# A ninth resident expert tile, and products of constants in TensorE's waits, in a four-stage transformer kernel

## The chip, the cores and the metric
One core of one Trainium2 chip runs the whole kernel in one launch. The metric is the time of an execution in microseconds, the median of several runs. Views of the trace count from the start of the profiled execution's span.

## The reference
Two blocks, in fp32, on 256 tokens of width 1024. The first has two layers, and each is a mixer and a mixture of experts:

```python
for layer in range(DEPTH):                       # DEPTH = 2
    h = rms_norm(x, norm_mix_g[layer])
    ...                                          # layer 0: even_mixer, layer 1: odd_mixer
    x = x + mix
    h = rms_norm(x, norm_ffn_g[layer])
    x = x + hier_moe(h, moe_w_group[layer], moe_b_group[layer], ...)
```

`hier_moe` picks one of 4 groups and the best 2 of its 8 experts for each token. There are 32 experts of hidden width 512 in a layer: silu(h W_gate) * (h W_up), times W_down, weighted by the gates. The second block has two layers of a hybrid mixer and a gated feed-forward part (hyb0, ffn0, hyb1, ffn1), and a last norm.

## The kernel before
The stages run one after another: even, moe0, odd, moe1, hyb0, ffn0, hyb1, ffn1, fin. Each engine has its own program, and semaphores with names such as "even mixed3" order them (`K.after(name)`). All weights stream from HBM through tiles of 128 x 4096 fp32 (2048 KB), in one fixed order (`chunk_table`), issued by SyncE (`sp_program`, L3270) strictly in turn: before a tile SyncE waits until the slot's last holder is free, and everything later in the order waits behind it.

An expert stage has 8 groups q of four experts. A group has 12 tiles, in this order: g{q}_0 to 3 (gate), u{q}_0 to 3 (up), d{q}_0 to 3 (down), so a stage has 96. Tile 0 is g0_0, tile 8 is d0_0, tile 95 is d7_3. The ring has six slots; while the ring goes round, a tile waits for the one six ring places ahead of it. Two tiles of each expert stage, g0_3 and u0_0, have places of their own at the end of the arena, the large work area, which is free only when the mixer before is nearly done (`aside`: "even mixed3", "odd z3"). The router's weights (`_r`) have another place.

For each group TensorE gathers the chosen tokens (at most 32 an expert) by a one-hot product (L804), multiplies gate and up tiles (L828, 16 matmuls a tile on quarters of the array), transposes, multiplies the down tiles (L853), and scatters the result back into x with four products (L860). Before group 0 comes the router: transposes of x (L717), logits (L785), a chain of small DVE operations that ends in "chosen", positions (L789 to L791), the first one-hot, and then gather(0). The PSUM banks go round in turn (`bank`).

An expert with more than 32 tokens is served by the general path (`over_pe` and its like), behind a branch at the end of the stage, which needs the normed features in `HT`. They are made in group 1 for every input, by `features_pe` and `features_act`.

After an expert stage the next norm transposes x (`norm_pe`, L641), and in hyb0 ACT cuts the first weights (L2323) before it copies the features (L2405).

Of the kernel before, what the change touches and what calls it, by code (L numbers as in the profile page):

```python
# [188 lines left out]
class Kernel:  # L189
    def __init__(self, nc, ctx, Wd, Pd, x_in, out_d, stages):  # L190
# [51 lines left out]
        for i, (name, k, n) in enumerate(self.chunks):  # L242
            if name in aside:
                area, landed, freed = aside[name]
                self.slot.append((landed, area[:, 0:k * n]))
                self.freed.append(freed)
                self.landing[name] = (landed, 16)
                continue
            if name == "moe0_g0_0":
                order, turn = [3, 4, 5, 2, 0, 1], 0  # L250
            elif name == f"moe1_g{NE // 4 - 1}_0":
                order, turn = [1, 3, 4, 2, 0, 5, 1, 2, 0, 4, 5, 3], 0
            elif i == first:
                order, turn = list(range(FEW)), 0
            s, turn = order[turn % len(order)], turn + 1
            was, nth = held.get(s, (None, 0))
            self.freed.append(was and "free " + was)
            if name == "moe0_g0_3" or (s == 2 and was == "lora"):
                self.freed[-1] = "even mixed3"
            held[s] = (name, nth + 1)  # L260
            r, o = (ring, s) if s < FEW else (ring2, s - FEW)
            self.slot.append((self.s_slot[s], r[:, o * SLOT:o * SLOT + k * n]))
            self.place[name] = s
            self.landing[name] = (self.s_slot[s], 16 * (nth + 1))
# [11 lines left out]
    def aside(self, sem):  # L276

        out = {}
        for st, before, done in (("moe0", "even", "even mixed3"), ("moe1", "odd", "odd z3")):
            if st in self.stages:  # L280
                done = done if before in self.stages else None
                for i in range(2):
                    at = NA - 2 * SLOT + i * SLOT
                    out[f"{st}_" + ("g0_3", "u0_0")[i]] = (self.AR[:, at:at + SLOT], sem(f"s_{st}_{i}"), done)
                r = self.CS_T[:, 1440:1728] if st == "moe0" else self.AR[:, 12300:12588]
                out[st + "_r"] = (r, sem(f"s_{st}_r"), done if st == "moe1" else None)
        return out
# [337 lines left out]

def norm_pe(K, pe, st):
    S, b, ident = K.sig[st, "pe"], norm_bufs(K, st), K.par("ident", 0, 128)
    of, p = K.high if K.stage_before(st) == "odd" else K.banks, {}
    for t in range(2):  # L630
        for k in range(0, 8, 2):
            name = f"{st} nT{k}"
            if t == 0:
                p[k] = bank(K, pe, name, of)
            if k == 0:
                pe.wait_ge(*K.after(f"{st} xv{t}"))
            elif k == 4:
# [36 lines left out]
def moe_bufs(K, st):  # L674
    b = norm_bufs(K, st)
    buf = Area(K.AR, b.end, s5_top())
    b.L = buf(2, 36)
# [6 lines left out]
    b.SQs = [buf(2, 4, CAP) for _ in range(2)]  # L684
    b.XGs = [buf(8, 4 * CAP) for _ in range(2)]
    b.SG = [buf(512) for _ in range(2)]
# [64 lines left out]

def features_pe(K, pe, st):

    S, b, ident = K.sig[st, "pe"], norm_bufs(K, st), K.par("ident", 0, 128)
    for k in range(0, 8, 2):
        p = bank(K, pe, f"{st} nT{k}")
        for kk in (k, k + 1):
            for t in range(2):
                o = (kk - k) * 256 + t * 128
                r = pe.transpose(p[:, o:o + 128], b.xn[:, t, kk * 128:(kk + 1) * 128], ident)  # L760
        r.then_inc(*S.up(f"{st} nT{k}"))

def features_act(K, a, st):
    S, g = K.sig[st, "act"], "g_" + st
    for k in range(0, 8, 2):
        p = K.banks[f"{st} nT{k}"]
        a.wait_ge(*K.after(f"{st} nT{k}"))
        for kk, names in ((k, []), (k + 1, [f"{st} nT{k} read"])):
            o = (kk - k) * 256  # L770
            a.activation(K.HT[:, kk, :], p[:, o:o + 256], ACT.Copy, scale=K.par(g, kk)).then_inc(*S.up(*names))

def moe_pe(K, pe, st):
# [5 lines left out]
    for t in range(2):  # L780
# [5 lines left out]
        r.then_inc(*S.up(f"{st} r{t}", f"free {st}_r"))  # L786
    p = bank(K, pe, st + " pos")
    pe.wait_ge(*K.after(st + " chosen"))
    pe.matmul(p[:, 0:32], tri, b.Sf[:, 0, :], start=True, stop=True)  # L789
# [22 lines left out]
    for q in range(NE // 4):  # L812
# [28 lines left out]
        if q < NE // 4 - 1:  # L841
            gather(q + 1)
        if q == 1:
            features_pe(K, pe, st)
        ys = [bank(K, pe, f"{st} y{q}{n}") for n in range(2)]
        pe.wait_ge(*K.after(f"{st} hT{q} read"))
        for k in range(4):
# [3 lines left out]
            for n in range(2):  # L851
                for j in range(4):
                    r = pe.matmul(ys[n][32 * j:32 * j + 32, :], b.HTr[u][:, k, j * CAP:(j + 1) * CAP],  # L853
                                  w[:, j, n * 512:(n + 1) * 512], start=k == 0, stop=k == 3)
            r.then_inc(*S.up("free " + name, f"{st} y{q}"))
        for t in range(2):
            for n in range(2):
                pe.wait_ge(*K.after(f"{st} y{q}{n} read"))
                p = bank(K, pe, f"{st} o{q}{n}{t}")
                pe.matmul(p, b.SC[u][:, t, :], b.YS[u][:, n, :], start=True, stop=True).then_inc(  # L860
# [4 lines left out]
def moe_act(K, a, st):  # L865
# [7 lines left out]
    for q in range(NE // 4):  # L873
# [6 lines left out]
        a.activation(b.SC[u], half2(K.banks[f"{st} sT{q}"][:, 0:256]), ACT.Copy).then_inc(*S.up(f"{st} sT{q} read"))  # L880
        if q == 1:
            features_act(K, a, st)
        next(beside, None)
# [197 lines left out]
def over_end(K, e, l):  # L1081
    dve, act, pe, _ = K.over[l]
    e.wait_ge(dve, 3 * NE)
    e.wait_ge(act, NE)
    e.wait_ge(pe, 8 * NE)

def over_pe(K, pe, st, l, flag, hint):
    b, (dve, act, done, dma), HT = over_bufs(K), K.over[l], K.HT
    with over_path(K, pe, st, "pe", flag, hint):  # L1090
        for e in range(NE):
            pe.wait_ge(dma, 16 * 12 * (e + 1))
# [19 lines left out]
def over_act(K, a, st, l, flag):  # L1112
    b, (dve, done, pe, dma) = over_bufs(K), K.over[l]
    with over_path(K, a, st, "act", flag):
        for e in range(NE):
            a.wait_ge(pe, 8 * e + 4)
            if e:
# [5 lines left out]
def over_dve(K, v, st, l, flag):  # L1123

    b, (done, act, pe, dma), G = over_bufs(K), K.over[l], kept_gates(K, l)
    with over_path(K, v, st, "dve", flag):
        for e in range(NE):
            v.wait_ge(act, e + 1)
            v.tensor_tensor(b.hi, K.ps[:, 4:8, 0:256], b.sg, MUL).then_inc(done, 1)
            for t in range(2):  # L1130
                v.wait_ge(pe, 8 * e + 6 + 2 * t)
                v.scalar_tensor_tensor(out=K.X[:, t, :], in0=K.ps[:, 2 * t:2 * t + 2, :].rearrange("p n d -> p (n d)"),
# [4 lines left out]
def over_sp(K, sp, st, l):  # L1137
    b, (dve, act, pe, dma) = over_bufs(K), K.over[l]
    first = K.index[st + "_g0_0"]
    with over_path(K, sp, st, "sp", over_flag(K, sp, st, l)):  # L1140
        for e in range(NE):
            q, j = e // 4, e % 4
            if e:
                sp.wait_ge(pe, 8 * e)
            for part, dst in ((0, b.wg), (4, b.wu), (8, b.wd)):
# [18 lines left out]
def even_bufs(K):  # L1164
    b, cv, buf = Box(), K.consts("even_c"), Area(K.AR)
    b.M = buf(14, 256)
    b.LD, b.AA, b.GG, b.KK = (buf(4, 256) for _ in range(4))
    b.OT, b.YT = buf(8, 256), buf(4, 256)
    b.R, b.K2, b.VV = b.M[:, 0:4, :], b.M[:, 4:8, :], b.M[:, 8:12, :]
# [16 lines left out]
    two.PT, two.PV, two.VS = b.R[:, 0, :], b.K2[:, 0, :], b.VV[:, 0, :]  # L1186
    two.bh_at, two.bh = 14 * 256 + 12 * 256, b.KK[:, 0, :]
    two.BS, two.CS = b.AA[:, 0, :], b.LD[:, 0, :]
# [2161 lines left out]
def pool_program(K, g):  # L3350
# [3 lines left out]
    for st in K.stages:  # L3354
        nxt = K.stage_after(st)
        if st[:3] in ("moe", "ffn") and nxt is not None and nxt + "_c" in K.coffs:
            before = K.stage_before(st)
            if before is not None:
                for sem, n in K.ends(before):
                    g.wait_ge(sem, n)  # L3360
            load_consts(K, g, nxt)

# [244 lines left out]
```

## Time and profile before

| | |
|---|---|
| median of 3 runs | 2744.92 us (2742.62 to 2747.47) |
| profiled execution, its own time | 2738.76 us |
| its span | 2737.0 us |
| TensorE (matmuls) busy | 2300.2 us, 84% |
| weight loads, DVE, ACT busy | 1749.6, 1263.6, 941.2 us |
| moved by DMA | 663.18 MB, 242 GB/s mean |
| mean granted TensorE clock | 0.936 of full speed |

A busy share is an average over stages: the expert stages lie at about 273 to 732 us and 910 to 1370 us of the span, and there the views of single stretches have to be read. A clock of 0.50 is 1.2 GHz, one of 1.00 is 2.4 GHz.

### The profile page before, as it was taken

The page shows a single profiled execution, that of the slowest core. Times are in us where ns is not written, and L with a number is a line of the kernel's source. Part 1 is how long each engine was busy: PE and PEld are TensorE (multiplying, and loading weights), DVE is VectorE, ACT ScalarE, POOL GpSimd, SP SyncE. Part 2 cuts the span into 40 slices and gives each one's busy share as a digit, 9 for nine tenths or more (in the row PEclk, how much of TensorE's full clock was granted, in tenths as well). Part 3 has the DMA queues.
Part 4 walks back from the last instruction along what each step waited for, and adds up shares of the span by engine and source line. Part 5 has one row for each costly group of instructions (what it writes and reads, how often), then busy time and mean ns, then how long its engine had stood idle before and what let it go on. Part 6 is the DMA issues. An engine that isn't in the chain of part 4 may idle for free.

```text
span 2737.0 us, 37411 instructions
## 1 busy us (share of the span) xinstructions
PE 2300.2 (84%) x16364; PEld 1749.6 (64%) x16364; DVE 1263.6 (46%) x1914; ACT 941.2 (34%) x1382; POOL 2.4 (0%) x8
## 2 busy tenths in 40 slices
PE   7877766666696866666599999999999999999999
PEld 6666322211274421122189998999979999989997
DVE  2575321222294211111066568765545656866554
ACT  3133100000113200000055557745444555764543
POOL 0000000000000000000000000000000000000000
PEclk9998888988897988878899999999999999999999
DMA  6101999999905599999954443445544434334452
GB/s 274 62 1 74 400 428 428 428 427 428 416 17 248 244 428 427 427 428 428 427 198 170 149 178 141 154 154 199 182 172 154 167 146 185 130 148 160 180 185 100
DMA packets 47818, 663.18 MB, mean 242 GB/s; under 512 B 5280, under 2 KB 5536, under 8 KB 7584
## 3 DMA queue, kind: packets, MB, share of 16 engines
q1 hardware_dynamic: 47072, 657.39, 59.7%
q8 instruction: 132, 2.16, 0.3%
q0 software_dynamic: 576, 3.32, 0.3%
q14 instruction: 38, 0.31, 0.0%
HBM read 659.64 MB, written 1.05 MB: 241 GB/s over the span
## 4 chain that ended last, share of the span: by engine, by line
PE 54%; DMA 29%; DVE 9%; ACT 7%; issue 2%; SPq 0%; DVEq 0%; ACTq 0%
DMA ring<-w_dram 28%; PE ps L2346 7%; PE ps L2348 7%; PE ps L2347 7%; PE ps L1818 3%; PE ps L1231 2%; PE ps L828 2%; PE ps L2599 2%; PE ps L2600 2%; PE ps L2601 2%; PE ps L853 2%; ACT r L2323 2%; PE ps L3201 1%; PE ps L3199 1%; PE ps L3200 1%
## 5 line engine op out<-in xcount | busy, mean ns | idle before, releaser
L2334 DVE TENSOR_TENSOR r<-ring,r 128x1024 fp32r<-128x1024 f32 (+1 forms) x392 | 505.1, 1301 | 345.9 <-ACT r L2323 345.3
L2346 PE MATMUL ps<-r 128*128 128x256 f32 x2112 | 608.0, 288 | 15.1 <-DVE arena L2933 5.7
L2347 PE MATMUL ps<-r 128*128 128x256 f32 x2112 | 598.2, 283 | 0.0
L2348 PE MATMUL ps<-r 128*128 128x256 f32 x2112 | 598.0, 283 | 0.0
L2323 ACT ACTIVATE r<-ring 128x1024 fp32r<-128x1024 f32 (+1 forms) x392 | 429.5, 1116 | 269.1 <-PE ps L2348 131.8
L828 PE MATMUL ps<-ring,arena 128*32 128x512 f32 x1984 | 297.4, 731 | 207.0 <-DMA ring<-w_dram 206.9
L2346 PEld LDWEIGHTS ps<-r 128*128 128x128 f32 x2112 | 405.5, 192 | 22.8 <-issue 6.7
L2347 PEld LDWEIGHTS ps<-r 128*128 128x128 f32 x2112 | 405.7, 192 | 0.2
L2348 PEld LDWEIGHTS ps<-r 128*128 128x128 f32 x2112 | 405.5, 192 | 0.0
L828 PEld LDWEIGHTS ps<-ring,arena 128*32 128x32 f32 x1984 | 62.1, 121 | 433.0 <-DMA ring<-w_dram 221.2
L1030 DVE TENSOR_TENSOR arena<-ps,arena 128x512 f32<-128x512 f32 x16 | 11.1, 692 | 472.7 <-PE ps L828 472.7
L853 PE MATMUL ps<-ring,arena 128*32 128x512 f32 x1024 | 145.4, 702 | 81.1 <-DMA ring<-w_dram 80.1
L2599 PE MATMUL ps<-arena,r 128*128 128x256 f32 x512 | 145.4, 284 | 0.0
L2600 PE MATMUL ps<-arena,r 128*128 128x256 f32 x512 | 143.9, 281 | 0.0
L853 PEld LDWEIGHTS ps<-ring,arena 128*32 128x32 f32 x1024 | 30.5, 119 | 177.2 <-DMA ring<-w_dram 121.8
L2601 PE MATMUL ps<-arena,r 128*128 128x256 f32 x512 | 143.8, 281 | 0.0
L878 ACT ACTIVATE arena<-ps 128x512 f32<-128x512 f32 x16 | 9.6, 597 | 292.9 <-PE ps L828 292.9
L880 ACT ACTIVATE arena<-ps 128x256 f32<-128x256 f32 x16 | 6.1, 383 | 285.4 <-PE ps L834 285.4
L885 ACT ACTIVATE arena<-ps 128x512 f32<-128x512 f32 x16 | 9.6, 597 | 262.7 <-PE ps L853 262.7
L1038 DVE COPY arena<-ps 128x512 f32<-128x512 f32 x16 | 11.1, 692 | 192.4 <-PE ps L853 192.4
L2599 PEld LDWEIGHTS ps<-arena,r 128*128 128x128 f32 x512 | 96.5, 188 | 1.2 <-issue 0.7
L2600 PEld LDWEIGHTS ps<-arena,r 128*128 128x128 f32 x512 | 96.5, 188 | 0.1
(433 smaller groups left out, 3416.6 us busy)
## 6 DMA issues: line engine op xcount, KB each, us to landing
ring<-w_dram SPq DMA_DIRECT2D x305, 2048.0 KB, 23.7
arena<-w_dram SPq DMA_DIRECT2D x4, 2048.0 KB, 21.9
ring<-w_dram SPq DMA_DIRECT2D x4, 1024.0 KB, 4.9
cst<-w_dram POOLq DMA_DIRECT2D x2, 973.0 KB, 8.2
x<-x_dram SPq DMA_DIRECT2D x1, 1024.0 KB, 7.9
ring<-w_dram SPq DMA_DIRECT2D x2, 512.0 KB, 13.5
out_dram<-x SPq DMA_DIRECT2D x4, 256.0 KB, 2.0
ring<-w_dram SPq DMA_DIRECT2D x1, 768.0 KB, 15.8
```

The costliest lines, as they stand in the source:

```text
L828: r = pe.matmul(p[32 * j:32 * j + 32, :], xg[:, k, j * CAP:(j + 1) * CAP], w[:, kk * 4 + j, :], start=k == 0, stop=k == 7)
L853: r = pe.matmul(ys[n][32 * j:32 * j + 32, :], b.HTr[u][:, k, j * CAP:(j + 1) * CAP], w[:, j, n * 512:(n + 1) * 512], start=k == 0, stop=k ...
L1231: x = pe.matmul(o(c), l[:, c, :], r(c), start=True, stop=True)
L1818: r = pe.matmul(p[:, n * 256:(n + 1) * 256], w[:, k, c0 + n * 128:c0 + n * 128 + 128], rhs[:, k, :], start=k == 0, stop=k == n_k - 1)
L2323: a.activation(hi, w, ACT.Copy).then_inc(*S.up(f"hi {s}"))
L2334: v.tensor_tensor(lo, w, hi.bitcast(F32), SUB).then_inc(*S.up(f"lo {s}", *(["free " + name] if last else [])))
L2346: pe.matmul(out, hi[:, k, :], K.HH[:, k, :], start=k == 0, stop=False)
L2347: pe.matmul(out, hi[:, k, :], K.HL[:, k, :], start=False, stop=False)
L2348: r = pe.matmul(out, lo[:, k, :], K.HH[:, k, :], start=False, stop=k == 7)
L2599: pe.matmul(o, hi[:, k, :], b.YH[:, kk, :], start=kk == 0 and n == 0, stop=False)
L2600: pe.matmul(o, hi[:, k, :], b.YL[:, kk, :], start=False, stop=False)
L2601: r = pe.matmul(o, lo[:, k, :], b.YH[:, kk, :], start=False, stop=kk == 15 and n == 1)
```

## The change
Each expert stage gets a third arena place, for u0_1. In moe0 it is free with the others; in moe1 it waits for "odd av3". To make room, the arena areas of the even stage are put in another order, and the gathered inputs `XGs` move from the arena to `HT`. The general path, which found its features in `HT`, makes them itself, and `features_pe` and `features_act` go. The router's weights of moe1 go to the space of the constants of the odd stage, behind "odd roped1", and GpSimd waits for the router's matmuls before it loads the constants of hyb0. The ring order of moe1's last group is another. `warm` multiplies the identity by constants into a bank that is written again later; it is called three times before "chosen", twice after each of the first three down tiles of the last group, and in the norms before the waits.

```diff
             elif name == f"moe1_g{NE // 4 - 1}_0":
-                order, turn = [1, 3, 4, 2, 0, 5, 1, 2, 0, 4, 5, 3], 0
+                order, turn = [2, 0, 1, 3, 4, 5, 2, 0, 1, 4, 5, 3], 0
...
-                for i in range(2):
-                    at = NA - 2 * SLOT + i * SLOT
-                    out[f"{st}_" + ("g0_3", "u0_0")[i]] = (self.AR[:, at:at + SLOT], sem(f"s_{st}_{i}"), done)
-                r = self.CS_T[:, 1440:1728] if st == "moe0" else self.AR[:, 12300:12588]
-                out[st + "_r"] = (r, sem(f"s_{st}_r"), done if st == "moe1" else None)
+                heads = "odd av3" if done == "odd z3" else done
+                for name, at, when in (("g0_3", NA - 2 * SLOT, done), ("u0_0", NA - SLOT, done), ("u0_1", NA - 3 * SLOT, heads)):
+                    out[f"{st}_{name}"] = (self.AR[:, at:at + SLOT], sem(f"s_{st}_{name}"), when)
+                r, when = (self.CS_T[:, 1440:1728], None) if st == "moe0" else (self.CS_T[:, 0:288], done and "odd roped1")
+                out[st + "_r"] = (r, sem(f"s_{st}_r"), when)
...
+def warm(K, pe, out):
+
+    n = out.shape[1]
+    pe.matmul(out, K.par("ident", 0, 128), K.par("ident", 0, n), start=True, stop=True)
...
@@ norm_pe
             if k == 0:
+                if t == 0 and K.stage_before(st):
+                    warm(K, pe, p[0][:, 0:512 if after_moe(K, st) else 256])
+                elif t and K.stage_before(st):
+                    warm(K, pe, p[6][:, 128:256])
+                    warm(K, pe, p[6][:, 384:512])
                 pe.wait_ge(*K.after(f"{st} xv{t}"))
...
@@ moe_bufs
-    b.XGs = [buf(8, 4 * CAP) for _ in range(2)]
+    b.XGs = [K.HT[:, i:i + 4, :].rearrange("p a (b c) -> p (a b) c", b=2) for i in (0, 4)]
...
@@ moe_pe
     p = bank(K, pe, st + " pos")
+    for _ in range(3):
+        warm(K, pe, p)
     pe.wait_ge(*K.after(st + " chosen"))
...
-        if q == 1:
-            features_pe(K, pe, st)
         ys = [bank(K, pe, f"{st} y{q}{n}") for n in range(2)]
+        if q == NE // 4 - 1:
+            spare = bank(K, pe, f"{st} o{q}00")
...
             r.then_inc(*S.up("free " + name, f"{st} y{q}"))
+            if q == NE // 4 - 1 and k < 3:
+                warm(K, pe, spare)
+                warm(K, pe, spare)
...
-                p = bank(K, pe, f"{st} o{q}{n}{t}")
+                p = spare if q == NE // 4 - 1 and t == n == 0 else bank(K, pe, f"{st} o{q}{n}{t}")
...
@@ moe_act
-        if q == 1:
-            features_act(K, a, st)
...
@@ over_pe
+        xn = norm_bufs(K, st).xn
+        for k in range(8):
+            for t in range(2):
+                r = pe.transpose(K.ps[:, k // 2, k % 2 * 256 + t * 128:k % 2 * 256 + t * 128 + 128],
+                                 xn[:, t, k * 128:(k + 1) * 128], K.par("ident", 0, 128))
+        r.then_inc(done, 1)
+        pe.wait_ge(act, 8)
...
@@ even_bufs
-    b.LD, b.AA, b.GG, b.KK = (buf(4, 256) for _ in range(4))
-    b.OT, b.YT = buf(8, 256), buf(4, 256)
+    b.OT = buf(8, 256)
+    b.LD, b.AA, b.GG = (buf(4, 256) for _ in range(3))
+    kk, b.KK, b.YT = buf.at, buf(4, 256), buf(4, 256)
...
@@ pool_program
+            if st == "moe1":
+                g.wait_ge(*K.after("free moe1_r"))
             load_consts(K, g, nxt)
```

## Rows read from the trace of the kernel before

**Rows 1.** The page, 40 equal slices of the span: rate of all DMA.

```profile
GB/s 274 62 1 74 400 428 428 428 427 428 416 17 248 244 428 427 427 428 428 427 198 170 149 178 141 154 154 199 182 172 154 167 146 185 130 148 160 180 185 100
```

**Rows 2.** The page, the chain that ended last, by line.

```profile
DMA ring<-w_dram 28%; PE ps L2346 7%; PE ps L2348 7%; PE ps L2347 7%; PE ps L1818 3%; PE ps L1231 2%; PE ps L828 2%; PE ps L2599 2%; PE ps L2600 2%; PE ps L2601 2%; PE ps L853 2%; ACT r L2323 2%; PE ps L3201 1%; PE ps L3199 1%; PE ps L3200 1%
```

**Rows 3.** The chain in order of time, moe0: start us, us, what.

```profile
343.96 1.97 PE ps L828 x16
345.94 27.34 DMA ring<-w_dram
...
728.06 3.59 PE ps L853 x16
```

**Rows 4.** Windows, moe0's start: busy us (instructions) by engine, clock, DMA share, GB/s.

```profile
288.00:290.00 2.00, 2.00 (x20) 1.39 (x22) 1.08 (x3) 0.00 (x0) 0.00 (x0) 1.00 0.18 74
290.00:292.00 2.00, 2.00 (x24) 0.65 (x20) 0.87 (x5) 0.00 (x0) 0.00 (x0) 1.00 0.00 0
292.00:294.00 2.00, 2.00 (x24) 0.62 (x20) 0.00 (x0) 0.00 (x0) 0.00 (x0) 1.00 0.98 254
```

**Rows 5.** Timeline of SyncE's DMA issues: start us, us, what, how many.

```profile
260.42 0.80 SPq L3270 DMA_DIRECT2D arena<-w_dram  x2
...
839.33 0.80 SPq L3270 DMA_DIRECT2D ring<-w_dram  x2
...
906.62 35.07 SPq L3270 DMA_DIRECT2D ring<-w_dram  x8
```

**Rows 6.** Timeline of the odd stage, "odd roped1" and "odd av3".

```profile
839.30 1.23 DVE L2134 TENSOR_TENSOR arena<-arena 128x1024 f32<-128x1024 f32 x1
...
887.77 0.39 PE L1926 MATMUL ps<-arena 128*128 128x128 f32 x2
```

**Rows 7.** Windows, the end of odd and moe1's start, columns as in rows 4.

```profile
884.00:906.00 22.00, 21.29 (x55) 9.84 (x54) 2.13 (x3) 8.45 (x15) 0.00 (x0) 1.00 0.00 0
...
916.00:918.00 2.00, 0.00 (x0) 0.00 (x0) 2.00 (x16) 0.21 (x1) 0.00 (x0) 0.50 1.04 439
...
920.00:922.00 2.00, 1.17 (x6) 1.19 (x6) 1.74 (x10) 0.01 (x1) 0.00 (x0) 0.50 0.34 141
922.00:924.00 2.00, 2.00 (x12) 2.00 (x11) 0.61 (x4) 0.00 (x0) 0.00 (x0) 0.50 0.00 0
...
926.00:928.00 2.00, 2.00 (x22) 1.61 (x24) 0.86 (x2) 0.00 (x0) 0.00 (x0) 1.00 0.00 0
928.00:930.00 2.00, 2.00 (x25) 0.55 (x20) 1.10 (x5) 0.00 (x0) 0.00 (x0) 1.00 0.03 8
930.00:932.00 2.00, 2.00 (x24) 0.62 (x20) 0.00 (x0) 0.00 (x0) 0.00 (x0) 1.00 0.81 188
```

**Rows 8.** Timeline, group 1 of moe0, then the start of moe1.

```profile
357.04 3.74 PE L804 MATMUL ps<-arena 128*128 128x128 f32 x32
...
361.25 3.02 ACT L771 ACTIVATE ring<-ps,pp 128x256 f32<-128x256 f32 x8 [4.79 <-PE ps L760]
...
918.55 0.61 PE L789 MATMUL ps<-arena,pp 128*128 128x32 f32 x2 [3.27 <-DVE arena L970]
...
920.84 6.23 PE L804 MATMUL ps<-arena 128*128 128x128 f32 x32 [0.83 <-issue]
...
927.37 5.36 PE L828 MATMUL ps<-ring,arena 128*32 128x512 f32 x48
```

**Rows 9.** Timeline, last tiles of moe0 and moe1, and the norm behind.

```profile
728.06 3.53 PE L853 MATMUL ps<-ring,arena 128*32 128x512 f32 x16 [2.97 <-DMA ring<-w_dram]
...
1360.89 1.92 PE L853 MATMUL ps<-ring,arena 128*32 128x512 f32 x16 [3.01 <-DMA ring<-w_dram]
1365.86 3.32 PE L853 MATMUL ps<-ring,arena 128*32 128x512 f32 x16 [3.04 <-DMA ring<-w_dram]
...
1376.40 2.73 PE L641 MATMUL ps<-pp,arena 128*128 128x128 f32 x12 [0.72 <-ACT arena L576]
...
1376.77 1.04 ACT L2323 ACTIVATE r<-ring 128x1024 fp32r<-128x1024 f32 x1
```

More of the change, by code:

```diff
@@ L675, in moe_bufs @@
     b = norm_bufs(K, st)
-    buf = Area(K.AR, b.end, s5_top())
+    buf = Area(K.AR, b.end, NA - 3 * SLOT)
     b.L = buf(2, 36)
@@ L749, in turn_act @@
     scale_act(K, a, st, 1)
[L752 to L771, printed above, removed]
 def moe_pe(K, pe, st):
@@ L1083, in over_end @@
     e.wait_ge(dve, 3 * NE)
-    e.wait_ge(act, NE)
-    e.wait_ge(pe, 8 * NE)
+    e.wait_ge(act, 8 + NE)
+    e.wait_ge(pe, 1 + 8 * NE)
 def over_pe(K, pe, st, l, flag, hint):
@@ L1114, in over_act @@
     with over_path(K, a, st, "act", flag):
+        a.wait_ge(pe, 1)
+        for k in range(8):
+            a.activation(K.HT[:, k, :], K.ps[:, k // 2, k % 2 * 256:k % 2 * 256 + 256], ACT.Copy,
+                         scale=K.par("g_" + st, k)).then_inc(done, 1)
         for e in range(NE):
-            a.wait_ge(pe, 8 * e + 4)
+            a.wait_ge(pe, 8 * e + 5)
             if e:
@@ L1127, in over_dve @@
         for e in range(NE):
-            v.wait_ge(act, e + 1)
+            v.wait_ge(act, e + 9)
             v.tensor_tensor(b.hi, K.ps[:, 4:8, 0:256], b.sg, MUL).then_inc(done, 1)
             for t in range(2):
-                v.wait_ge(pe, 8 * e + 6 + 2 * t)
+                v.wait_ge(pe, 8 * e + 7 + 2 * t)
                 v.scalar_tensor_tensor(out=K.X[:, t, :], in0=K.ps[:, 2 * t:2 * t + 2, :].rearrange("p n d -> p (n d)"),
@@ L1142, in over_sp @@
             q, j = e // 4, e % 4
-            if e:
-                sp.wait_ge(pe, 8 * e)
+            sp.wait_ge(pe, 8 * e + 1)
             for part, dst in ((0, b.wg), (4, b.wu), (8, b.wd)):
@@ L1186, in even_bufs @@
     two.PT, two.PV, two.VS = b.R[:, 0, :], b.K2[:, 0, :], b.VV[:, 0, :]
-    two.bh_at, two.bh = 14 * 256 + 12 * 256, b.KK[:, 0, :]
+    two.bh_at, two.bh = kk, b.KK[:, 0, :]
     two.BS, two.CS = b.AA[:, 0, :], b.LD[:, 0, :]
```

## The prediction
> **What bounds the kernel now.** I read the page first. Its line of DMA rates shows 428 GB/s, the highest figure of the line, in slices 6 to 10 and 15 to 20: the two expert stages [rows 1]. The chain that ended last names the transfers into the ring as its largest single item, 28% of the span [rows 2]. The chain in order of time shows why: through an expert stage it goes from a tile's landing to some 2 us of matmuls, which free a ring slot, and from that slot to the landing of the tile that takes it, 27.34 us and six tiles later [rows 3]. The matmuls of tile 17 of the first expert stage start at 343.96, those of the last, tile 95, at 728.06: 384.10 / 78 = 4.92 us for one tile of 2048 KB. So an expert stage ends when its last tile lands, plus a tail. Its length is the number of tiles left to stream when streaming begins, times 4.92 us. Outside these stages the rate is far below 428, and there a tile can be fetched for nothing.
>
> Then I looked at how each stream begins. With windows of 2 us, moe0's shows a hole: 74 GB/s at 288 to 290, nothing until 292, 254 after it [rows 4]. Counting what is missing from 428, the hole is 2 x (354 + 428 + 174) / 428 = 4.47 us. All free slots are full, and tile 8 waits for the slot of tile 0, which TensorE has only just begun to read. In moe1 the hole is larger: 141, then 0, 8 and 188 GB/s between 920 and 932 [rows 7], or 2 x (287 + 3 x 428 + 420 + 240) / 428 = 10.4 us.
>
> **The ninth tile.** Before, six ring slots and two arena slots hold tiles 0 to 7 when the stage begins. After, tile u0_1 has an arena slot of its own, so tile 8 (d0_0) gets a ring slot whose holder was done before the stage.
>
> moe0: the new slot is free with "even mixed3", the event at which SyncE issues the two arena tiles at 260.42 [rows 5]; the tile for the last slot goes once even_out1 is used. Its 4.9 us of transfer follow the eighth tile's and fill a hole of 4.47 us. Tile 9 then waits for tile 0's slot, as tile 8 did, and finds it free while the ninth tile is still on its way. The stream gains what the hole is worth: 4.47 us. An earlier release of the slot adds nothing here, as no hole is left.
>
> moe1: the router's weights move from the arena to the space of the cosines and wait for "odd roped1". The DVE operation behind that name starts at 839.30 and takes 1.23 us [rows 6]; SyncE issues the two odd_out tiles, which are queued ahead, at 839.33 [rows 5], and they keep the DMA busy for 9.8 us, so that this wait and all tiles queued behind it cost nothing. The ninth slot waits for "odd av3", and the two matmuls before it start at 887.77 [rows 6]. Everything behind u0_1 in SyncE's queue (u0_2, u0_3, d0_0, d0_1) waits with it. From 884 to 906 the DMA moves nothing [rows 7], so u0_1 and u0_2 are in by about 898; u0_3 and d0_0 follow the slots of the odd_out tiles from 906.62 on [rows 5], where two tiles went before. The hole stays where it is, and one tile fewer comes after it: 4.92 us. The constants of hyb0, which GpSimd now holds back until the router's matmuls are over (about 4 us), share the DMA ahead of the hole; at 128 x 1946 x 4 bytes, 1.0 MB, they need 2.3 us of it.
>
> **What is removed.** The general path's own transposes and copies take 16 transposes and 8 ACT operations out of group 1 of each expert stage, and the gathered inputs move to the buffer that they used. Group 1 lies in the middle of the DMA stream, where TensorE waits some 3 us for each tile: 0. If the stream were no cover, it would be worth the 3.02 us of the copies [rows 8] a stage; no part of the general path runs in this profile. The changed order of ring slots in moe1's last group asks each tile to wait for one at least five places ahead (four before): 0.
>
> **The products of constants.** One such product, 128x512, should cost what a 128x512 pass of the tiles' matmuls suggests: 48 matmuls that use a quarter of the array together take 5.36 us [rows 8], four side by side 0.45 us, so 0.45 us at full clock and twice that at half. All stand in front of a wait. Three ahead of "chosen": TensorE idles 3.27 us there [rows 8], they need 1.3 to 2.7. Two after each of the last group's first three down tiles: a wait of some 3 us [rows 9], they need 0.9 to 1.8. A tile's 16 matmuls take 1.8 us at full clock (5.36 / 3) and 3.6 at half, and 3.6 + 1.8 = 5.4 is over 4.92: if the clock stayed down, each tile would delay the next by 0.5, or 1.4 us a stage. In the norms they need 0.2 to 0.9 us beside idle time of the same size: 0, at worst 0.5 us in all.
>
> Can they pay? In moe1 the clock is 0.50 from 916 to past 922 and 1.00 from 926 on [rows 7]. In this time the 32 gather matmuls (L804) take 6.23 us; the same 32 of a later group take 3.74 [rows 8]. Up to 2.5 us earlier, tile 0's slot is free, the hole in moe1 ends, and the whole stream with it. But three products end 2 us before "chosen" at full clock, and whether they hold the clock up until then no row shows; I take 1.0, with 0 and 2.5 as bounds. In the tails, the last tile's 16 matmuls take 3.53 us (moe0) and 3.32 (moe1), against 1.92 for the tile at 1360.89 [rows 9]: the clock fell in the 3 us of waiting. This time is behind the last landing and fully exposed, 1.6 + 1.4 = 3.0 us. Here the products cut the idle stretch from 3 to 2 us at full clock, and at half clock they leave hardly any, so that the clock should be up at the last tile more often than not; I take 2.0 of 3.0, bounds 3.0 and -2.8 (the delay above). After the tail, moe1's twelve slow transposes (2.73 us) end while ACT is still busy with the first cut (1.04 us from 1376.77) and what follows it in order [rows 9]: 0.
>
> The Trainium skill, "TensorE: Matmul & The Clock Gate", section "HAM oscillation — how this bites in real kernels", describes this pattern: matmuls shorter than the wait for the next slice lose the clock and each burst starts slow. The trace agrees in part: [rows 9] has both a fast and a slow burst after the same wait. By that page alone all 3.0 us of the tails would be there to win, and the sum would be 1.0 us larger.
>
> **The sum.** 4.47 + 4.92 + 1.0 + 2.0 = 12.4 us off the profiled execution, whose own time is 2738.76 us (span 2737.0). That execution is 6.2 us below the median of the three runs, 2744.92, and 3.9 below the fastest; tile counts and holes don't depend on it, so I take 12.4 off the median: 2732.5.
>
> **Rivals.**
> *The transfers alone pay.* What holds the clock is not what the products do, or it starts at another place in each execution and the profiled one was an unlucky one. For it: in [rows 7] the clock stays at 0.50 through 922 to 924, in which TensorE is busy all the time. 4.47 + 4.92 = 9.4 us: 2735.5. The same page, section "Part 1: The HAM clock gate (the "warmup" mystery)", says that the number of slow matmuls varies between runs of one kernel, which is this rival's rule.
> *The tile pays in one stage only.* In one stage its load doesn't move the first landing after the hole (in moe1 because the queue behind "odd av3" runs late; that costs from 909 on, when 4 tiles at 4.9 us and 2.3 us of constants no longer end by 931; in moe0 because the fifth and sixth transfers slip). 888 is 21 us ahead of that. Gain 4.5 to 5 us plus 0 to 3: about 2738.5, at the edge of what can be measured.
> *Slower: the stream itself loses pace.* Place: the 174 tiles after the holes. One more part of the arena is written while DVE and ACT use the rest, and a tile that takes longer shifts everything behind it. Price: 174 x 0.1 = 17.4 us, 8 us slower on balance; it decides from 0.054 us a tile (4.92 to 4.974) where the gain of 9.4 is gone. Against it: the rate is the same 427 to 428 in every slice of both stages, with tiles going to ring and arena alike [rows 1]. 2753.
>
> **How the numbers follow.** Forecast (transfers plus some of the clock): 0.60. Transfers alone: 0.24. One stage only: 0.10. More of the clock than its bound in the profile: 0.03. Slower stream: 0.03. Low end: 9.4 + 2.5 + 3.0 = 14.9 us gives 2730.0; the runs of before lie up to 2.5 us from their median, and with the rare fourth case I go to 2726.5. High end: the transfers alone less 2.8 us of delays is 2738.3, and 1.7 of scatter (both extremes together are rare) makes 2740, which also takes in most of the one-stage case. 0.2% is 5.5 us, about what a measurement of this kernel can tell from no change. Faster by more: the first, second and fourth case, and a little of the third: 0.88. Within it: 0.09. Slower: 0.03.
>
> **What would show it.** In windows of 2 us, 288 to 294 must have the full rate in moe0; in moe1 a hole must remain, 8 to 10 us long, with nine tiles ahead of it, and two more tiles must move between 888 and 898. The last tile of moe0 must start some 4.5 us earlier after its stage's start, that of moe1 5 to 7 us. Gather matmuls near 3.7 us and last tiles near 1.9 would show the products at work. If the router's matmuls start as before and the last landing isn't earlier, the first step is wrong; if all is as described and the total isn't, a later stage gave it back.

## The result and the profile after

The changed kernel takes 2726.8 us (median of 4 runs, 2725.96 to 2727.97), the kernel before 2743.77 us beside it (4 runs, 2742.6 to 2747.47): a ratio of 0.9936, with a 95% interval of 0.9919 to 0.9953. The profiled execution takes 2726.56 us, 12.2 less than the profiled one of before (2738.76). The forecast took 12.4 us off the earlier median of 2744.92, for 2732.5; the median fell by 17.0 against the one beside it.

First the page of the kernel after: the rate of DMA in 40 slices and the chain by line, for [rows 1, 2].

```profile
GB/s 276 62 1 78 427 428 428 427 428 427 399 16 241 303 428 428 428 427 428 428 177 155 159 186 124 155 177 179 186 170 155 184 130 186 141 138 166 175 186 101
DMA ring<-w_dram 27%; PE ps L2349 7%; PE ps L2350 7%; PE ps L2351 7%; PE ps L819 3%; PE ps L1821 3%; PE ps L1234 2%; PE ps L2602 2%; PE ps L2603 2%; PE ps L2604 2%; PE ps L844 2%; ACT r L2326 1%; PE ps L3204 1%; PE ps L3202 1%; PE ps L3203 1%
```

The expert stages run at the same 427 to 428 GB/s, and the transfers into the ring are still the largest item. The windows of the two starts, for [rows 4, 7] with the same columns:

```profile
286.00:288.00 2.00, 2.00 (x24) 0.65 (x20) 0.94 (x5) 0.00 (x0) 0.00 (x0) 1.00 1.02 434
288.00:290.00 2.00, 2.00 (x24) 0.56 (x20) 0.00 (x0) 0.00 (x0) 0.00 (x0) 1.00 1.02 434
290.00:292.00 2.00, 2.00 (x24) 0.61 (x20) 0.00 (x0) 0.00 (x0) 0.00 (x0) 1.00 1.00 418
292.00:294.00 2.00, 2.00 (x24) 0.65 (x20) 0.00 (x0) 0.60 (x1) 0.00 (x0) 1.00 0.99 418
...
880.00:890.00 10.00, 9.86 (x27) 4.63 (x26) 0.75 (x1) 6.03 (x8) 0.00 (x0) 1.00 0.89 349
...
916.00:918.00 2.00, 1.99 (x18) 2.00 (x19) 1.64 (x10) 0.00 (x0) 0.00 (x0) 1.00 0.00 0
918.00:920.00 2.00, 2.00 (x21) 2.00 (x19) 0.84 (x2) 0.00 (x0) 0.00 (x0) 1.00 0.03 8
920.00:922.00 2.00, 2.00 (x22) 0.75 (x25) 1.81 (x6) 0.00 (x0) 0.00 (x0) 1.00 0.00 0
922.00:924.00 2.00, 2.00 (x24) 0.52 (x16) 0.00 (x0) 0.00 (x0) 0.00 (x0) 1.00 0.61 123
924.00:926.00 2.00, 2.00 (x24) 0.65 (x20) 0.00 (x0) 0.00 (x0) 0.00 (x0) 1.00 0.94 369
```

In moe0 the hole of 288 to 294 is gone. In moe1 a hole remains: from 914 to 926 what is missing from 428 adds up to 9.1 us. And the DMA moves 4.2 MB, two tiles, between 880 and 892, in a stretch where before it moved nothing (the odd stage begins some 7 us earlier now, so these times answer to 887 and later in [rows 7]). TensorE's timeline, for [rows 8, 9]; L630 is `warm`, L795 the gather, L819 the gate and up tiles, L844 the down tiles, L854 the scatter:

```profile
275.18 4.52 PE L630 MATMUL ps<-pp 128*128 128x512 f32 x6
279.54 0.30 PE L780 MATMUL ps<-arena,pp 128*128 128x32 f32 x2
...
281.11 3.81 PE L795 MATMUL ps<-arena 128*128 128x128 f32 x32 [0.82 <-issue]
...
721.55 1.92 PE L844 MATMUL ps<-ring,arena 128*32 128x512 f32 x16 [1.06 <-DMA ring<-w_dram]
...
733.88 1.35 PE L1849 MATMUL ps<-ring 128*128 128x256 f32 x5 [1.22 <-ACT ring L675]
...
901.83 1.91 PE L728 MATMUL ps<-pp,x 128*128 128x128 f32 x16
904.87 4.99 PE L774 MATMUL ps<-cst,ring 128*128 128x36 f32 x32 [1.13 <-DVE arena L893]
909.67 4.93 PE L630 MATMUL ps<-pp 128*128 128x512 f32 x6
914.43 0.30 PE L780 MATMUL ps<-arena,pp 128*128 128x32 f32 x2
...
916.01 3.81 PE L795 MATMUL ps<-arena 128*128 128x128 f32 x32 [0.82 <-issue]
...
1353.88 1.92 PE L844 MATMUL ps<-ring,arena 128*32 128x512 f32 x16 [1.04 <-DMA ring<-w_dram]
1356.52 3.70 PE L854 MATMUL ps<-arena 128*128 128x512 f32 x8 [0.72 <-ACT arena L877]
1362.95 1.13 PE L630 MATMUL ps<-pp 128*128 128x512 f32 x2 [2.73 <-issue]
```

The gather and both last tiles run at full clock (3.81, 1.92, 1.92 us). Two waits are new. The router's matmuls of moe1 (L774) wait 1.13 us for a DVE operation of the odd stage, and the first projection of odd (L1849) 1.22 us for ACT. Before, neither waited for these:

```profile
740.75 1.53 PE L1846 MATMUL ps<-ring 128*128 128x256 f32 x6 [0.40 <-DVE ring L653]
...
909.86 1.92 PE L717 MATMUL ps<-pp,x 128*128 128x128 f32 x16
911.62 3.66 PE L785 MATMUL ps<-arena,ring 128*128 128x36 f32 x32
```

And at 1362.95 TensorE has idled 2.73 us with "issue" as the reason: it waited for nothing that the profile shows.

**By stages.** The points are starts on TensorE's timeline: T a stage's first transposes, g0 tile 0's matmuls, "last" the last down tile, "next" the first matmul after the norm behind it. "even" runs from the landing of x to moe0's T. Each cell is in us from the profile of that execution. The expert sum is the four columns T to last and last to next of both stages.

| execution | span | even | moe0 T-g0 | T-last | last-next | moe1 T-g0 | T-last | last-next | expert sum |
|---|---|---|---|---|---|---|---|---|---|
| before | 2737.0 | 262.5 | 17.44 | 456.35 | 12.69 | 17.51 | 456.00 | 14.14 | 939.2 |
| before_again | 2742.9 | 267.1 | 17.33 | 455.94 | 12.75 | 17.52 | 456.84 | 14.23 | 939.8 |
| before_look1 | 2738.5 | 262.5 | 17.44 | 456.53 | 12.61 | 17.48 | 456.31 | 14.45 | 939.9 |
| before_look2 | 2743.5 | 267.1 | 17.75 | 456.56 | 13.17 | 17.48 | 456.07 | 14.28 | 940.1 |
| after | 2724.7 | 262.5 | 15.28 | 451.62 | 12.33 | 18.28 | 452.05 | 13.67 | 929.7 |
| changed_again | 2726.4 | 263.1 | 14.39 | 450.48 | 12.33 | 18.31 | 452.23 | 15.08 | 930.1 |
| changed_look1 | 2729.4 | 262.2 | 14.39 | 451.92 | 12.32 | 19.93 | 453.59 | 13.68 | 931.5 |
| changed_look2 | 2732.6 | 266.4 | 14.38 | 451.37 | 12.33 | 19.94 | 453.49 | 14.05 | 931.2 |

On the mean of four executions each, the expert stages gain 939.7 - 930.6 = 9.1 us: 5.0 in moe0's stream, 0.5 behind it, 3.5 in moe1's stream, 0.2 behind it. The spans gain 12.2. Of the other 3.1 us, 0.4 lie in the load of x, 1.2 in even, 0.1 in odd and 1.3 behind moe1's "next", where the changed kernel has products in three more norms.

### The profile page after: what moved, and what is told of

Read it like the earlier page. It is cut to its first block, busy times and chain, and to the rows that moved or that the text cites. A ratio compares the mean times of both kernels' runs of the same rounds, so it can differ in the third digit from the quotient of the medians.

```text
span 2724.7 us, 37455 instructions
## 1 busy us (share of the span) xinstructions
PE 2313.3 (85%) x16398; PEld 1750.2 (64%) x16398; DVE 1263.5 (46%) x1914; ACT 935.1 (34%) x1366; POOL 2.4 (0%) x8
## 4 chain that ended last, share of the span: by engine, by line
PE 55%; DMA 27%; DVE 9%; ACT 7%; issue 2%; DVEq 0%; SPq 0%; ACTq 0%
DMA ring<-w_dram 27%; PE ps L2349 7%; PE ps L2350 7%; PE ps L2351 7%; PE ps L819 3%; PE ps L1821 3%; PE ps L1234 2%; PE ps L2602 2%; PE ps L2603 2%; PE ps L2604 2%; PE ps L844 2%; ACT r L2326 1%; PE ps L3204 1%; PE ps L3202 1%; PE ps L3203 1%
## 5 line engine op out<-in xcount | busy, mean ns | idle before, releaser
L819 PE MATMUL ps<-ring 128*32 128x512 f32 x1952 | 300.1, 747 | 197.6 <-DMA ring<-w_dram 194.4
L819 PEld LDWEIGHTS ps<-ring 128*32 128x32 f32 x1952 | 62.2, 124 | 425.6 <-DMA ring<-w_dram 210.2
L844 PE MATMUL ps<-ring,arena 128*32 128x512 f32 x1024 | 141.2, 684 | 73.0 <-DMA ring<-w_dram 70.8
L844 PEld LDWEIGHTS ps<-ring,arena 128*32 128x32 f32 x1024 | 30.1, 117 | 166.0 <-DMA ring<-w_dram 111.6
```

Of the source, the lines that this page charges most:

```text
L819: r = pe.matmul(p[32 * j:32 * j + 32, :], xg[:, k, j * CAP:(j + 1) * CAP], w[:, kk * 4 + j, :], start=k == 0, stop=k == 7)
```

## The experiments

**Parts alone.** transfers_only leaves out all products of constants:

```diff
-    for _ in range(3):
-        warm(K, pe, p)                     # before "chosen"
...
-                warm(K, pe, spare)         # twice, last group
...
-                    warm(K, pe, ...)       # in norm_pe, all
```

> The changed kernel with all products of constants taken out (router, last group, norms); ninth tile, places and ring order as changed. It tells the transfers from the clock. If the transfers pay as in the prediction (4.5 + 4.9 us) and a later start of the router and of odd costs some 2 us (theory below on PSUM banks), it runs 7 to 8 us under the kernel before, about 2736, and 9 us over the changed one. Rival, the transfers are all of the gain: within 2 us of the changed kernel, 2727. Rival, the transfers pay only as the prediction has it and nothing is lost: 2734.5.

products_only keeps them and takes the ninth tile back into the ring, with the old order of the last group:

```diff
-... ("u0_0", NA - SLOT, done), ("u0_1", NA - 3 * SLOT, heads)):
+... ("u0_0", NA - SLOT, done)):
```

> The changed kernel with u0_1 back in the ring, so eight tiles are resident as before, and the ring order of the last group of moe1 as before; the products stay. If the clock pays what is left of 17 us after the transfers, 7 to 8 us under the kernel before, 2736. The earlier release of tile 0's slot (2 to 3 us) counts in both stages here, as both have a hole. If the products pay only the 3 us of the prediction: 2741.

Measured: transfers_only 2738.51 us (11 runs), ratio 0.9978 (0.9967 to 0.9988); products_only 2740.11 (11 runs), 0.9993 (0.9984 to 1.0002). By the medians of the same comparison (before 2741.93) they are 3.4 and 1.8 us under the kernel before, not 7 to 8; by the interval the transfers are worth 3.3 to 9.0 us, and the products alone aren't told from nothing. Their profiles' expert sums are 936.9 and 937.5, 2.8 and 2.2 us under before, against 9.1 for both. The profiled execution of transfers_only is the slowest of its 11 (2742.47). In moe0 it has tile 0's matmuls no earlier (17.74 us after T) and gains 2.1 us of stream; with the products they come 2.5 to 3.4 earlier (14.4 to 15.3 in the changed kernel). Of the 4.1 us by which the two parts fall short of the whole, 3.1 are in its moe0 tail, last to next 15.93 us instead of 12.8. Its timeline (L837 down tiles, L844 scatter):

```profile
729.57 3.64 PE L837 MATMUL ps<-ring,arena 128*32 128x512 f32 x16 [1.85 <-DMA ring<-w_dram]
733.93 6.20 PE L844 MATMUL ps<-arena 128*128 128x512 f32 x8 [0.72 <-ACT arena L867]
...
1368.52 1.92 PE L837 MATMUL ps<-ring,arena 128*32 128x512 f32 x16 [1.30 <-DMA ring<-w_dram]
```

The granted clock was 0.50 from 728 to 738, through moe0's last tile and most of the scatter (6.20 us instead of 3.70), while moe1's last tile took 1.92 us with no product near it.

**The turn of the PSUM banks.** `features_pe` took four turns of `bank` in each expert stage. Without them every bank behind group 1 is another one. banks_back turns the counter on and does nothing else:

```diff
             gather(q + 1)
+        if q == 1:
+            K.banks.n += 4
         ys = [bank(K, pe, f"{st} y{q}{n}") for n in range(2)]
```

> The changed kernel, and the turn of PSUM banks moved on by four at group 1 of each expert stage, where the removed transposes took four. Theory: without these four turns the first bank of odd's inputs is that of the norm's last quarter and the router's first bank in moe1 is that of the last transposes of x, so both wait for a copy that they don't need: 0.8 us in odd, 1.1 us in moe1, and up to 1.3 us more where the router's matmuls then run at the lower clock. 2 to 3 us under the changed kernel, 2724.5, and the router of moe1 follows its transposes at once. Rival, banks don't matter since the copies are waited for anyway: no difference, 2727.

Measured: 2729.19 us (5 runs), 0.9953 (0.994 to 0.9967). Its timeline at the starts of odd (L1851) and of moe1:

```profile
735.71 3.69 PE L1851 MATMUL ps<-ring 128*128 128x256 f32 x16 [0.40 <-DVE ring L664]
...
905.37 1.92 PE L728 MATMUL ps<-pp,x 128*128 128x128 f32 x16
907.13 3.66 PE L774 MATMUL ps<-cst,ring 128*128 128x36 f32 x32
910.62 2.82 PE L630 MATMUL ps<-pp 128*128 128x512 f32 x6
913.97 0.41 PE L780 MATMUL ps<-arena,pp 128*128 128x32 f32 x2 [0.53 <-DVE arena L963]
...
915.65 5.44 PE L795 MATMUL ps<-arena 128*128 128x128 f32 x32 [0.82 <-issue]
```

Both new waits are gone. The router follows its transposes after 1.76 us instead of 3.05 and keeps the full clock (3.66 us instead of 4.99), T-g0 is 16.02 instead of 18.3 to 19.9, moe1's T-last 449.60, and last-next behind moe0 is 11.51 instead of 12.33. Counting the calls of `bank` says whose it was: in the changed kernel the router's first bank is one that the stage's own transposes had just filled, and L1849's one of the norm's (L652); before and in banks_back, each had another holder. The turn alone undoes both waits. It doesn't make the kernel clearly faster: the forecast 2724.5 was missed, the expert sum is 928.0 (2.6 under the changed kernel's mean), and in moe1 the gather took 5.44 us here, behind three products.

**The products of the norms.** no_norm_products takes the three `warm` calls out of `norm_pe`, and banks_no_norm does so with the banks turned back:

```diff
-                if t == 0 and K.stage_before(st):
-                    warm(K, pe, p[0][:, 0:512 if after_moe(K, st) else 256])
-                elif t and K.stage_before(st):
-                    warm(K, pe, p[6][:, 128:256])
-                    warm(K, pe, p[6][:, 384:512])
```

> The changed kernel without the products in the norms. If they only get in the way of the transposes (0.45 us behind moe0, as the trace of the changed kernel suggests), 0.5 to 1.5 us faster over five norms, 2726. Rival, they hold the clock for the projections behind a norm: 1 to 4 us slower, and the granted clock behind the norm is lower.

> Four bank turns put back in group 1, and no products in the norms. By the stages of the two profiles before it: odd starts 0.8 + 0.4 us earlier, moe1's first tile 1 to 2.3 us earlier, hyb0 0.9 to 2.4 us earlier than in the changed kernel, 3 to 5 us in all, and it beats both kernels. Rival, the norm products hold the clock behind moe1: hyb0 starts later than with them.

Measured: 2730.57 us (6 runs), 0.9962 (0.995 to 0.9974), and 2728.43 (5 runs), 0.995 (0.9936 to 0.9963). Behind moe0 last-next is 11.89 without them and 12.33 with, and 11.07 against 11.51 with the banks back: they cost 0.44 us there both times. Behind moe1 it is 12.77 and 12.91 without, 13.67 to 15.22 with: there they cost 0.8 us or more, with the stall below present in all of these. Behind moe1's "next" the sign is the other way. The nine profiles with products in the norms last 1356.6 to 1358.5 us from there to the end (mean 1357.4), the nine without 1357.0 to 1359.5 (mean 1358.8). That is 1.3 us in their favour; whether they cause it, no run was built to tell. The totals can't tell these sizes from nothing.

**The products before "chosen".** two_router_products has two instead of three (banks back, none in the norms); no_router_products is the changed kernel without them:

```diff
-    for _ in range(3):
+    for _ in range(2):      # two_router_products; no_router_products: none
         warm(K, pe, p)
```

> As banks_no_norm, and two products instead of three ahead of the wait for the chosen experts. Three of them take 2.8 us at full clock and 4.5 to 5.5 where the clock falls in them, against a wait of 3.3 us, so that they delay the positions by up to 2 us. If two (1.9 us, or 3 to 3.7) still hold or bring back the clock: up to 1.5 us faster than with three in moe1, where the hole is. If not, the gather runs at 0.50 and moe1's first tile comes 1 to 2 us later.

> The changed kernel without the three products ahead of the wait for the chosen experts. If they hold the clock for the gather: from the start of the router's transposes to the first tile 17.5 us or more in moe0 (15.3 with them) and 20 in moe1 (18.3), the last tile of moe1 1.5 to 2 us later, moe0's 0 to 2 us later since its hole is closed. Rival, the gather's clock doesn't depend on them: no difference in either.

Measured: 2728.84 us (5 runs), 0.9952 (0.9938 to 0.9965), and 2730.76 (5 runs), 0.9963 (0.995 to 0.9977). The timelines, two_router_products first (moe1; L790 is the gather):

```profile
903.82 3.66 PE L769 MATMUL ps<-cst,ring 128*128 128x36 f32 x32
907.31 3.29 PE L630 MATMUL ps<-pp 128*128 128x512 f32 x4
910.66 0.64 PE L775 MATMUL ps<-arena,pp 128*128 128x32 f32 x2
...
912.60 3.81 PE L790 MATMUL ps<-arena 128*128 128x128 f32 x32 [0.82 <-issue]
```

and no_router_products (moe0; L793 is the gather):

```profile
278.23 0.61 PE L778 MATMUL ps<-arena,pp 128*128 128x32 f32 x2 [3.28 <-DVE arena L960]
...
280.52 6.11 PE L793 MATMUL ps<-arena 128*128 128x128 f32 x32 [0.82 <-issue]
```

Here the gather takes 6.11 us without products and 3.81 with two, and nothing is delayed: moe1's T-g0 is 14.63, and the stage's T-last 448.37, the shortest of all with all_but_stalls. Over all 18 profiles the gather takes 5.3 to 6.5 us in each of the 12 stages that have no products ahead of it, and 3.81 in 22 of the 24 that have them. The two others are moe1 in banks_back (5.44) and moe0 in all_but_stalls (two products):

```profile
284.57 5.14 PE L790 MATMUL ps<-arena 128*128 128x128 f32 x32 [0.82 <-issue]
```

So the products hold the clock as a rule, not always. Three products of six records take 2.82 us at full clock, 0.94 each, and 4.5 to 5.5 where the clock is low in them; the wait is 3.3, and behind the slow ones the positions start 0.9 to 1.8 us late. In moe1 this gives back what the gather wins: no_router_products has a T-last of 452.18 there, no later than the changed kernel's 452.05 to 453.59, against the 1.5 to 2 us expected.

**The last group's products.**

```diff
-            if q == NE // 4 - 1 and k < 3:
-                warm(K, pe, spare)
-                warm(K, pe, spare)
```

> The changed kernel without the six products in the last group of each expert stage. Where the clock is low behind the last landing, the last tile takes 3.5 us instead of 1.9 and the eight scatter matmuls 6.2 instead of 3.7, as behind moe0 without any products: up to 4 us a stage, 2 us on average, 4 us slower in all than the changed kernel. Rival, as in the profile of before, where only the tile was slow: 1.5 us a stage at most. Rival, the products only cost time: no slower.

Measured: 2727.44 us (5 runs), 0.9955 (0.9941 to 0.9968). The end of moe1 (L844 down tile, L851 scatter):

```profile
1353.46 2.81 PE L844 MATMUL ps<-ring,arena 128*32 128x512 f32 x16 [2.97 <-DMA ring<-w_dram]
1356.97 5.78 PE L851 MATMUL ps<-arena 128*128 128x512 f32 x8 [0.70 <-ACT arena L874]
```

The last tile takes 2.81 us instead of 1.92 and the scatter 5.78 instead of 3.70, but last-next is 15.55 against 13.7 to 15.1: 3.0 us are lost in the two rows and at most 1.9 of them at the end, because the stall at "issue" isn't there: the norm's products follow the scatter at once. Behind moe0 there is no difference: the last tile took 1.92 us and last-next 12.33 without the products. The forecast of 4 us missed; the expert sum is 931.2 against 930.6. In the 12 profiles that have these products all 24 last tiles took 1.92 us; without them the eight of before took 3.3 to 3.6, and of the four in the two variants two took 1.92.

**The stall at "issue".** The branch over the general path stands between scatter and norm, and TensorE marks the place of its hint at the start of the stage's last group (L806). hint_late marks it just before the last scatter; all_but_stalls adds the banks, two router products and none in the norms:

```diff
-            flag, hint = over_flag(K, pe, st, l), pe.mark_branch_hint_location()
+            flag = over_flag(K, pe, st, l)
...
+        if q == NE // 4 - 1:
+            hint = pe.mark_branch_hint_location()
         for t in range(2):
             for n in range(2):
                 pe.wait_ge(*K.after(f"{st} y{q}{n} read"))
```

> The changed kernel with TensorE's branch hint marked behind the last down tile of an expert stage instead of at the start of its last group. In every kernel that has products in the last group, TensorE stands for 1.2 to 2.9 us with nothing to wait for between the scatter products and the norm behind moe1 (2.7 us in the changed kernel), and not in the kernels without them. 
> Ninth tile and last-group products as changed, four bank turns put back, no norm products, two products ahead of the chosen experts, hint marked late. If each piece is worth what its stage showed: some 6 us under the changed kernel, 2722. If the late hint does harm, 2 to 4 us over that.

Measured: 2734.78 us (6 runs), 0.997 (0.9957 to 0.9982), and 2728.16 (5 runs), 0.9941 (0.9927 to 0.9954). The norm behind each expert stage in hint_late:

```profile
735.45 1.13 PE L630 MATMUL ps<-pp 128*128 128x512 f32 x2 [2.80 <-issue]
...
1370.61 1.13 PE L630 MATMUL ps<-pp 128*128 128x512 f32 x2 [2.81 <-issue]
```

Now the stall stands behind both stages, where the changed kernel has it behind moe1 only (2.7 to 3.1 us in all four profiles). The theory fell and the second rival came true: the later mark brings the stall to the other branch too. all_but_stalls, at 2728.16 instead of the 2722 expected, has it in both tails too, without the name. Its norm's transposes start 7.07 us behind moe0's scatter (5.17 behind moe1's in the kernel before), and the idle time is put down to a DVE operation:

```profile
736.22 1.95 PE L647 MATMUL ps<-pp,arena 128*128 128x128 f32 x16 [3.37 <-DVE arena L609]
```

Since only the place of the mark was moved, the stall hangs on the branch and its hint. The Trainium skill, "Runtime: NRT & Kernel Launch", section "Instruction fetch mechanics", says that a taken branch to code outside the present window forces a fetch before execution goes on. A stall of 2.8 us at the branch fits this; that it is a fetch, no run shows. Behind moe1 all 12 profiles with products in the last group have it, and none of the others: the four of before, transfers_only and no_last_group_products don't. So in moe1 it came with these products. Why it came there and not in moe0 is open.

**Both kernels again.** changed_again, before_again, and two looks at each are the same kernels with no edit but empty lines at the end.

> The changed kernel once more, word for word, beside its variants on the same chip. If the first four runs of it (12 to 17 us under the kernel before) stood for it: 15 to 17 us under. If they were lucky draws of the even stage, whose length differs by up to 5 us between profiled executions of the same instructions: 11 to 13 us under, as its profiled execution is under that of before.

> The kernel before, word for word, for a second profiled execution. If the first profiled execution was a lucky draw: a span of 2740 to 2745, with the clock at 0.50 in at least one more place (router, scatter products behind a last tile, or the even stage) than in the first. Rival, its medians lie above its profile for a reason outside the span: the same stage lengths again, within 1 us.

> The changed kernel, one more execution with its profile. Theory A (the length of the even stage, which no part of the change touches, is drawn anew in each execution and by the same odds in both kernels): from the end of the load of x to the first transposes of moe0 either 262 to 263 us or 265 to 268. Theory B (the changed kernel always gets the short one): 262 to 263. The stretch from moe0's to hyb0's start, less the odd stage, should be 929.5 to 930.5 us by both.

> The kernel before, one more execution. Theory A: even stage 262 to 263 or 265 to 268 us with the same odds as in the changed kernel. Theory B: 265 to 268 in most executions (the first profile of before had 262.5, the second 267.1). Its two expert stages together some 9.5 us longer than those of the changed kernel by both theories.

> As the first of these looks at the changed kernel: 262 to 263 us for the even stage by theory B, either length by theory A.

> As the first of these looks at the kernel before: either length by theory A, 265 to 268 us more often than not by theory B. If both kernels show both lengths, the median gap beyond the 9.5 us of the expert stages is scatter of few runs.

Measured: changed_again 2727.88 us (5 runs), 0.9951 (0.9938 to 0.9965); before_again 2740.93 (11 runs) against 2744.9 for the same kernel in the same comparison, 0.9991 (0.9982 to 1.0). The median of changed_again is 13.2 us under the 2741.08 beside it, nearer the 11 to 13 expected of lucky draws in the first runs than 15 to 17. The profile of before_again is 5.9 us longer than the first of before, 4.6 of it in even. The looks, one execution each: changed 2731.19 and 2734.36, before 2740.28 and 2745.33. The changed ones' expert sums, 931.5 and 931.2, lie over the 929.5 to 930.5 expected, as moe1's T-g0 is 19.9 in them. Windows of the even stage in the four looks, changed_look1:

```profile
140.00:160.00 20.00, 17.15 (x249) 15.58 (x247) 14.04 (x45) 5.29 (x16) 0.00 (x0) 1.00 0.01 1
```

changed_look2:

```profile
140.00:160.00 20.00, 17.15 (x202) 15.67 (x203) 13.00 (x43) 4.73 (x14) 0.00 (x0) 0.83 0.00 1
```

before_look1:

```profile
140.00:160.00 20.00, 17.15 (x243) 15.44 (x243) 14.32 (x46) 5.29 (x16) 0.00 (x0) 1.00 0.01 1
```

before_look2:

```profile
140.00:160.00 20.00, 17.15 (x198) 15.57 (x197) 12.99 (x42) 4.35 (x13) 0.00 (x0) 0.80 0.00 1
```

One look at each kernel has the full clock at 140 to 160 and an even stage of 262.2 to 262.5 us, the other 0.80 or 0.83 there, 198 to 202 matmuls instead of 243 to 249, and 266.4 to 267.1. Both lengths occur in both kernels, so theory B fell and the length is drawn by the execution; whether the odds are equal, eight profiles can't say.

## Why the prediction came out as it did

The transfers were forecast rightly in kind. Four steps failed: what is removed was put at 0, a product was priced at half its cost, the clock's two terms (1.0 and 2.0) were paid back in other waits, and a gain in the stages was taken for the gain in the median. The first three left the expert stages with a gain of 9.1 us instead of 12.4; the last hid this behind a median that fell by 17.0.

**What bounds the kernel, and the ninth tile in moe0: as predicted in kind.** The windows have the full rate in 286 to 294. Of 4.47 us forecast, the stream gained 5.0 with the products. Without products before "chosen" it was 3.8 (no_router_products) and 2.1 (transfers_only) against before's profile, one profile each. So "an earlier release of the slot adds nothing here" was wrong: tile 0's slot, free some 2 to 3 us earlier, carries 1 us or more of it. Why transfers_only reached only 2.1 is partly open: its rate dips to 352 to 401 GB/s from 296 to 302, worth 0.7 us.

**The ninth tile in moe1: right.** The hole remained, 9.1 us long, and one tile fewer came after it. (The sign that a last tile 5 to 7 us earlier after the stage's start was to give didn't come, because of the next terms: it was 3.5 us.) The stage's length obeys 4.92 us less whatever T-g0 grew: after 4.92 - 0.77 = 4.15, measured 3.95; banks_back 4.92 + 1.49 = 6.41, measured 6.40; transfers_only 4.92 - 2.73 = 2.19, measured 2.08; products_only 0 - 0.81, measured -0.89; two_router_products 4.92 + 2.88 = 7.80, measured 7.63. The router's weights, the queue behind "odd av3" and the constants of hyb0 cost nothing that these sums leave room for.

**"What is removed: 0": the step that failed first.** It looked at the time of the removed instructions and not at what they did to names handed out in turn. The removal turned the banks by four, which cost 0.8 us at odd's start and, in moe1, 1.3 us of wait plus the clock that was lost in it: the router's 32 matmuls took 4.6 to 5.9 us instead of 3.66.

**The gather's clock: forecast +1.0, came -1.6.** The gather did win 2.4 us (6.23 to 3.81). But T-g0 grew from 17.5 to a mean of 19.1. In the first profile (+0.8) the bank wait took 1.3 us, the slower router 1.3 and the products' overrun 1.3, and 3.1 came back from the positions to tile 0. The products' cost was the second failed term: 0.45 us each, from matmuls that fill the array by quarters, against 0.94 measured at full clock. "They need 1.3 to 2.7" was 2.8 to 5.5 in a wait of 3.3. With the banks back and two products the term would have been 17.5 - 14.6 = +2.9.

**The tails: forecast 2.0 of 3.0, came 0.6.** The last tiles took 1.92 us in every profile that had the last group's products, against 3.3 to 3.6 before: 1.6 and 1.4 us were won, all of the 3.0. Of this, 0.8 in moe0 went back to odd's bank wait and 0.44 to the norm's products, and in moe1 1.3 to the stall at "issue" (the norm's first instruction 6.43 us behind the scatter's start instead of 5.17). "0, at worst 0.5" for the norms was too low: 0.44 behind moe0 and 0.8 or more behind moe1, with perhaps 1.3 won in the later stages.

**The sum.** The forecast's terms by what they measured: 5.0 (moe0) + 3.5 (4.92 less the late start, 1.4 to 1.6) + 0.6 (tails) = 9.1 us, in place of 12.4. That the profiled pair differed by 12.2, almost the forecast, is luck: 9.5 in the expert stages, 1.8 in the load of x and 1.2 in odd, less 0.2 behind. The gap of the medians, 17.0 in the first comparison and 13.2 in the second, holds these too: an even stage 4 to 5 us longer came in two of four profiles of before and in one of four of the changed kernel. How much of the 17.0 such draws explain, eight profiles can't say. The forecast mapped a gain in one execution onto a median of three runs, and took for granted that the other stages would be drawn alike.

**The rivals.** Transfers alone, by its own time, was wrong: without the products they bring 0.22% (0.12 to 0.33), not 9.4 us. Its reason has two halves. The profiled execution of before was no unlucky one: in all four, both last tiles took 3.3 to 3.6 us and both gathers 6.1 to 6.5. But a last tile can be fast with no product near it: transfers_only's took 3.64 and 1.92 us. One stage only: both paid. Slower stream: the rate is unchanged. More than the bound: the median looks like it, the stages don't.

Three versions have clearly shorter expert stages than the changed kernel: 923.6 us (two_router_products, span 2722.2), 924.4 (banks_no_norm) and 925.4 (all_but_stalls), against 930.6. The medians of the first two, 2728.84 and 2728.43, don't stand out from changed_again's 2727.88 in the same comparison, and all_but_stalls' ratio of 0.9941 doesn't from 0.9951. They aren't shown to be faster.

## What to carry to other kernels

Before an operation is costed at nothing because it is removed, look for what is handed out in turn behind it (banks, slots, semaphore counts): the next users get other holders, and a wait can appear in another stage. Filler matmuls belong in a wait only with their measured full-array cost at the low clock, and only as many as end before it. Compare a change of some 0.3% by the sum of the stages it touches in several profiles; the total carries draws of other stages as large as the change.

## What the hardware showed that was not expected

An fp32 product of 128x128 weights with 128x512, which fills the array, costs 0.94 us at full clock (2.82 for three) and counts as two records. Four quarter-array matmuls side by side took 0.45.

A stall of 2.6 to 3.1 us at a branch in TensorE appears or vanishes with the products in the group before it and with the place of the branch hint; where the profile says "issue", no wait that it shows stands in it, and in the changed kernel it took back most of the tail's gain in moe1.

The even stage, whose work is the same in both kernels, lasts 262.0 to 263.1 us or 265.0 to 267.6 in the 18 profiles. It has the short length in all nine where the window of 140 to 160 has a granted clock of 1.00 and the long one in all nine where that is 0.79 to 0.87.
